# Attention by pairs of heads, with turned tiles by key block and the reciprocal applied at the gate

## The reference

```python
s_loc = einsum(qb, kb) * scale          # 8 heads of 64, blocks of 128 queries, 3 neighbouring blocks of 128 keys
s_loc = where(|qpos - kpos| <= 128 and key exists, s_loc, -1e30)
s_ctx = einsum(qb, kc) * scale          # 256 context keys
p = softmax(concatenate([s_loc, s_ctx, sink_l]))     # one sink value per head
o = einsum(p[..., :nloc], vb) + einsum(p[..., nloc:nloc + nctx], vc)
total = total + gates * ((ys[i] * silu(zs[i])) @ w_os[i])   # o is ys[0], silu(zs[0]) the attention gate
```

## Time and profile before

| | us |
|---|---|
| median of 3 runs | 2764.37 |
| lowest and highest | 2763.32, 2779.56 |
| the profiled execution | 2763.59 |
| its span, first to last instruction | 2761.8 |
| TensorE busy in it | 2550.7 (92%) |
| VectorE, ScalarE, GpSimd busy | 1139.5, 1114.2, 1355.2 |
| context attention, about 99 to 125 us | 26 |
| first latent attention, about 549 to 697 us | 148 |
| second latent attention, about 1752 to 1900 us | 148 |

### The profile page before, as it was taken

The page is one execution under the profiler, slowest core; times in us unless marked ns, Lnnn a source line. Parts: engine busy times, 40 slices in busy tenths (PEclk is TensorE's granted clock), DMA queues, the critical chain, the costliest instruction groups (busy, mean ns, idle before and its releaser), DMA issues.

```text
span 2761.8 us, 39510 instructions
## 1 busy us (share of the span) xinstructions
PE 2550.7 (92%) x13009; PEld 2117.8 (77%) x13009; DVE 1139.5 (41%) x1692; ACT 1114.2 (40%) x2229; POOL 1355.2 (49%) x1052
## 2 busy tenths in 40 slices
PE   7888968988999989999999979888999899999997
PEld 2777967787888767777888867777888688888886
DVE  2453346377153432333344366483344323233332
ACT  2644553277221454434433343574213433343332
POOL 1657962266221258864655442464222455555553
PEclk9899989999999999999999999999999999999999
DMA  5345661100121145543433431000210343344333
GB/s 229 96 117 175 190 191 50 42 1 1 47 65 33 32 126 160 158 139 126 148 108 107 144 114 43 16 1 28 61 40 24 89 120 109 109 133 146 113 107 121
DMA packets 392336, 266.44 MB, mean 96 GB/s; under 512 B 16263, under 2 KB 361495, under 8 KB 390683
## 3 DMA queue, kind: packets, MB, share of 16 engines
q1 hardware_dynamic: 379552, 231.26, 28.3%
q10 hardware_dynamic: 12668, 33.67, 3.4%
HBM read 255.42 MB, written 9.45 MB: 96 GB/s over the span
## 4 chain that ended last, share of the span: by engine, by line
PE 73%; issue 10%; POOL 7%; DVE 6%; ACT 3%; DMA 0%; ACTq 0%; POOLq 0%; DVEq 0%; SPq 0%
PE ps L639 71%; POOL w_lo L549 6%; DVE a_probT_lo L1532 2%; PE ps L786 1%; ACT a_probT_hi L1254 1%; DVE a_out_sum L1532 1%; DVE norm_tmp L1677 0%; DVE x_post L2074 0%; DVE hT_lo L1532 0%; PE ps L671 0%; DMA w_ada<-in_w_ada 0%; DVE r_prev L1873 0%; PE ps L738 0%; ACT a_prob L1243 0%; DVE x_post L1636 0%
## 5 line engine op out<-in xcount | busy, mean ns | idle before, releaser
L549 POOL TENSOR_TENSOR w_lo<-w_raw,w_hi 128x512 fp32r<-128x512 f32 x834 | 1126.3, 1361 | 1104.7 <-ACT w_hi L1081 1096.2
L639 PE MATMUL ps<-hT_hi,w_hi 128*128 128x512 f32 (+1 forms) x2528 | 948.0, 375 | 56.9 <-POOL w_lo L549 33.5
L1081 ACT ACTIVATE w_hi<-w_raw 128x512 fp32r<-128x512 f32 x834 | 519.0, 629 | 1029.2 <-PE ps L639 863.9
L639 PE MATMUL ps<-hT_hi,w_lo 128*128 128x512 f32 (+1 forms) x2528 | 934.2, 370 | 0.0
L639 PE MATMUL ps<-hT_lo,w_hi 128*128 128x512 f32 (+1 forms) x2528 | 934.2, 370 | 0.0
L639 PEld LDWEIGHTS ps<-hT_hi,w_hi 128*128 128x128 f32 x2528 | 483.3, 191 | 154.3 <-POOL w_lo L549 35.4
L639 PEld LDWEIGHTS ps<-hT_hi,w_lo 128*128 128x128 f32 x2528 | 483.4, 191 | 79.2
L639 PEld LDWEIGHTS ps<-hT_lo,w_hi 128*128 128x128 f32 x2528 | 484.0, 191 | 75.6
L1532 DVE TENSOR_TENSOR merge_tmp<-merge_tmp,ps 128x512 f32<-128x512 f32 (+1 forms) x160 | 101.5, 634 | 694.8 <-PE ps L639 437.7
L587 POOL TENSOR_TENSOR a_prob<-a_prob,softmax_stats 128x640 f32<-128x640 f32 (+2 forms) x144 | 163.5, 1135 | 142.8 <-DVE softmax_stats L1788 142.4
L1532 DVE TENSOR_TENSOR merge_tmp<-merge_tmp 128x512 f32<-128x512 f32 (+1 forms) x120 | 165.2, 1377 | 4.1
(11 more groups left out here) (243 smaller groups left out, 2804.0 us busy)
## 6 DMA issues: line engine op xcount, KB each, us to landing
w_raw<-in_w_in SPq DMA_DIRECT2D x512, 256.0 KB, 2.9
w_raw<-in_w_o_rest SPq DMA_DIRECT2D x120, 256.0 KB, 2.9
w_raw<-in_w_out SPq DMA_DIRECT2D x80, 256.0 KB, 2.8
w_ada<-in_w_ada SPq DMA_DIRECT2D x8, 1536.0 KB, 9.5
w_raw<-in_w_ada SPq DMA_DIRECT2D x48, 256.0 KB, 2.8
w_raw<-in_w_o_attn SPq DMA_DIRECT2D x40, 256.0 KB, 2.9
w_raw<-in_dft_x SPq DMA_DIRECT2D x32, 256.0 KB, 2.7
gate_row<-gate_rows ACTq DMA_DIRECT2D x5, 512.0 KB, 3.6
```

The lines of the kernel that those rows point to most:

```text
L549: eng.tensor_tensor(w_lo[:, r, :], raw[:, r, :], w_hi[:, r, :].bitcast(F32), ALU.subtract).then_inc(sem["w_split"], tally.up("w_split"))
L639: return eng.matmul(dst, lhsT, rhs, start=start, stop=stop)
L1081: return eng.activation(dst, src, func, **kw)
```

## The change

Pairs of heads take the place of single steps for everything behind the exponential. The probabilities are no longer scaled. The turned tiles of a pair go by key blocks into three banks: bank 4 holds blocks 0 and 1 of both heads, bank 5 blocks 2 and 3, and bank 6 block 4, where there is one. Each bank is called a chunk c, with its own semaphores (pT_turned, pT_high, pT_low) from TensorE to ScalarE to VectorE and back. VectorE writes the reciprocal of each row sum 64 times side by side (`one_over`, 128 columns for a pair), TensorE turns that tile into the other half of bank 6 (`turn_over`), ScalarE copies it out (`save_over`), and GpSimd multiplies it into the gate tile (weighed), and then the attention result (gated), two instructions of 128x256 for every two pairs. The values are multiplied one pair later than before. The low part of chunk 2 waits for `save_over` of its own pair too.

```diff
@@ -244,6 +244,8 @@
         o_sum = at("a_out_sum", [P, 2, 2, P], W + 17928)
+        over = [at("a_one_over_rows", [P, 4, P], C + 512), at("a_one_over_rows_ctx", [P, 4, P], W + 4096)]
+        over_cols = [at("a_one_over", [P, 2, P], C + 1024), at("a_one_over_ctx", [P, 2, P], W + 4608)]
         kc = at("a_kT_ctx", [P, 2, 2, CTX], Z + 2048, F32R)
@@ -389,17 +392,21 @@
             return [c for k in range(p.NT // 2) for c in (k, p.NT - 1 - k)]
-        def turned_at(n, count):
...
+        def key_blocks(p, qb):
+            return 2 if p.ctx else 5 - (qb == 0) - (qb == p.NT - 1)
+        def chunk(p, qb, c):
+            return max(min(key_blocks(p, qb) - 2 * c, 2), 0)
+        def heads_of(g):
+            return slice(2 * (g % 2), 2 * (g % 2) + 2)
+        def turned_chunk(c, blocks):
+            return ps[:, 4 + c, 0:blocks * 2 * P].rearrange("p (j h n) -> p j h n", h=2, n=P)
         def results(p, b):
@@ -570,25 +577,15 @@
             def attention(p):
-                groups = p.NT * 2
...
+                for g in range(p.NT * 2):
                     pair, qb = g // (p.NT // 2), 2 * (g % (p.NT // 2))
-                    eng.wait_ge(sem["out_sum"], tally.take("out_sum"))
                     zz = z_pass[p.s][:, qb // p.TB, Z_A + pair, (qb % p.TB) * P:(qb % p.TB + 2) * P].rearrange(
                         "p (a n) -> p a n", n=P)
+                    eng.wait_ge(sem["over_saved"], tally.take("over_saved", 2))
+                    eng.tensor_tensor(zz, over[p.s][:, heads_of(g), :], zz, ALU.mult).then_inc(sem["weighed"], tally.up("weighed"))
+                    eng.wait_ge(sem["weighed"], tally.now("weighed"))
+                    eng.wait_ge(sem["out_sum"], tally.take("out_sum"))
                     eng.tensor_tensor(zz, o_sum[:, g % 2, :, :], zz, ALU.mult).then_inc(sem["gated"], tally.up("gated"))
-
...
             def retention(p):
@@ -772,51 +769,67 @@
                     mm(ps[:, c + 1, 0:CTX], q, kc[:, kv, 1, :], False, True).then_inc(sem["score"], tally.up("score"))
-                def turn(n):
...
+                pairs, probs = len(steps) // 2, tally.now("prob")
+                def turn_over(g):
+                    eng.wait_ge(sem["one_over"], tally.take("one_over"))
+                    if tally.now("over_turned"):
+                        eng.wait_ge(sem["over_saved"], tally.now("over_turned"))
+                    if tally.now("pT_turned2"):
+                        eng.wait_ge(sem["pT_low2"], tally.now("pT_turned2"))
+                    eng.transpose(ps[:, 6, 2 * P:3 * P], over_cols[p.s][:, g % 2, :], ident[:, :]).then_inc(
+                        sem["over_turned"], tally.up("over_turned"))
+                def turn(g, c):
+                    blocks = chunk(p, steps[2 * g][0], c)
+                    if not blocks:
+                        return
+                    eng.wait_ge(sem["prob"], probs + 2 * g + 2)
+                    if tally.now(f"pT_turned{c}"):
+                        eng.wait_ge(sem[f"pT_low{c}"], tally.now(f"pT_turned{c}"))
+                    dst = turned_chunk(c, blocks)
+                    for j in range(blocks):
+                        for hh in range(2):
+                            w = slice((2 * c + j) * P, (2 * c + j + 1) * P)
+                            last = eng.transpose(dst[:, j, hh, :], prob[:, 2 * (g % 2) + hh, w], ident[:, :])
+                    last.then_inc(sem[f"pT_turned{c}"], tally.up(f"pT_turned{c}"))
+                def values(g, c):
+                    qb, h = steps[2 * g]
                     lo, hi = window(qb)
-                    places = turned_at(n, hi - lo + 2)
...
+                    kv, count = h // 4, hi - lo + 2
+                    if not chunk(p, qb, c):
+                        return
+                    if c == 0 and g % 2 == 0:
                         if tally.now("out_sum"):
                             eng.wait_ge(sem["out_sum"], tally.now("out_sum"))
                         tally.skip("out_sum", 1)
-                    dst, heads = ps[:, 7, pair * 2 * P:(pair + 1) * 2 * P], slice(2 * pair, 2 * pair + 2)
...
+                    eng.wait_ge(sem[f"pT_low{c}"], tally.take(f"pT_low{c}"))
+                    dst = ps[:, 7, g % 2 * 2 * P:(g % 2 + 1) * 2 * P]
+                    for j in range(2 * c, 2 * c + chunk(p, qb, c)):
                         v = vx[:, lo + j, kv, :, :] if j < hi - lo else vc[:, j - (hi - lo), kv, :, :]
-                        mm(dst, v, pT_hi[:, j, heads, :], j == 0, False)
...
+                        mm(dst, v, pT_hi[:, j, heads_of(g), :], j == 0, False)
+                        last = mm(dst, v, pT_lo[:, j, heads_of(g), :], False, j == count - 1)
+                    if g % 2 and 2 * c + chunk(p, qb, c) == count:
                         last.then_inc(sem["pv"], tally.up("pv"))
                 eng.wait_ge(sem["a_split"], tally.take("a_split"))
-                scores(0)
...
+                for g in range(pairs + 3):
+                    if g < pairs:
+                        scores(2 * g)
+                    if g > 2:
+                        values(g - 3, 0)
+                        values(g - 3, 1)
+                    if g < pairs:
+                        scores(2 * g + 1)
+                    if g > 2:
+                        values(g - 3, 2)
+                    if 0 < g <= pairs:
+                        turn_over(g - 1)
+                        turn(g - 1, 2)
+                        turn(g - 1, 0)
+                        turn(g - 1, 1)
             def late_keys(p):
@@ -1246,13 +1259,21 @@
                         sink_column(n + 2)
-                def save(n):
...
+                weighed = tally.now("weighed")
+                def save(g, c):
+                    blocks = chunk(p, steps[2 * g][0], c)
+                    if blocks:
+                        eng.wait_ge(sem[f"pT_turned{c}"], tally.take(f"pT_turned{c}"))
+                        eng.activation(pT_hi[:, 2 * c:2 * c + blocks, heads_of(g), :], turned_chunk(c, blocks), ACT.Copy).then_inc(
+                            sem[f"pT_high{c}"], tally.up(f"pT_high{c}"))
+                def save_over(g):
+                    eng.wait_ge(sem["over_turned"], tally.take("over_turned"))
+                    if g > 3:
+                        eng.wait_ge(sem["weighed"], weighed + g // 2 - 1)
+                    act(over[p.s][:, g % 4, :], ps[:, 6, 2 * P:3 * P]).then_inc(sem["over_saved"], tally.up("over_saved"))
                 def low_half():
@@ -1269,16 +1290,21 @@
                 sink_column(1)
-                exps(0)
...
+                pairs = len(steps) // 2
+                for g in range(pairs + 3):
+                    if g < pairs:
+                        exps(2 * g)
+                    if g > 2 and g % 2 == 0:
                         low_half()
-                save(len(steps) - 1)
...
+                    if 0 < g <= pairs:
+                        save(g - 1, 2)
+                    if g < pairs:
+                        exps(2 * g + 1)
+                    if 0 < g <= pairs:
+                        save(g - 1, 0)
+                        save_over(g - 1)
+                        save(g - 1, 1)
+                tally.skip("weighed", pairs // 2)
             def decay_tables():
@@ -1782,19 +1807,25 @@
                         sem["max"], tally.up("max"))
-                def one_over(n):
...
+                turned, saved = tally.now("over_turned"), tally.now("over_saved")
+                def one_over(g):
+                    eng.wait_ge(sem["prob"], tally.take("prob", 2))
+                    if g > 1:
+                        eng.wait_ge(sem["over_turned"], turned + g - 1)
+                    eng.reciprocal(over_cols[p.s][:, g % 2, :].rearrange("p (h d) -> p h d", d=HD),
+                                   soft[:, heads_of(g), 1:2].to_broadcast([P, 2, HD])).then_inc(sem["one_over"], tally.up("one_over"))
+                def low(g, c):
+                    blocks = chunk(p, steps[2 * g][0], c)
+                    if blocks:
+                        eng.wait_ge(sem[f"pT_high{c}"], tally.take(f"pT_high{c}"))
+                        if c == 2:
+                            eng.wait_ge(sem["over_saved"], saved + g + 1)
+                        high = pT_hi[:, 2 * c:2 * c + blocks, heads_of(g), :].bitcast(F32)
+                        tt(pT_lo[:, 2 * c:2 * c + blocks, heads_of(g), :], turned_chunk(c, blocks), high, ALU.subtract).then_inc(
+                            sem[f"pT_low{c}"], tally.up(f"pT_low{c}"))
                 def add_halves(g):
@@ -1813,20 +1844,24 @@
                    vc[:, :, :, 0, :].bitcast(F32), ALU.subtract).then_inc(sem["a_split"], tally.up("a_split"))
-                groups = len(steps) // 4
...
+                pairs, groups = len(steps) // 2, len(steps) // 4
+                for g in range(pairs + 3):
+                    if 1 < g <= pairs + 1:
+                        low(g - 2, 2)
+                    if g < pairs:
+                        maximum(2 * g)
```

(67 more changed lines are left out.)

45 lines of the change are left out of this document (2 added, 43 removed).

## The result

The changed kernel takes 2832.47 us (median of 4 runs, 2822.72 to 2836.01), the kernel before 2763.85 us (4 runs, 2762.47 to 2779.56). The ratio is 1.0229, with a 95% interval of 1.0185 to 1.0274: slower, and the forecast of 2831 us is met within 2 us. The profiled execution is the fastest of the four, 2822.7 us; the other three, at 2831 to 2836 us, have a mean granted clock of 0.966 to 0.967 in place of 0.973. So the profile shows 59 of the 69 us.

What follows compares the result with a forecast made beforehand. No engine was full; a closed ring through VectorE and ScalarE, 5.69 us a pair, was to bound the changed kernel. 54 + 6 + 4 + 3 = +67 on 2763.6 us gave 2831 us, own range 2808 to 2850, 8-in-10 range 2788 to 2862.

Steps and rivals of the forecast that it cites:

- The stall before and what could be won: Latent passes before the change: 0.7 us of stall a pair, 45 us over 64 pairs, all that better overlap can win.
- The reciprocal's price: VectorE's reciprocal, widened from 1 to 128 columns, takes 0.95 us.
- The ring: VectorE's low parts, maxima and reciprocal, then ScalarE's exponential and copies, back to chunk 2's low part: 5.69 us a pair.
- The columns: Each column of 8 pairs in the latent passes takes 42.5 us against 35.7: +54 us in all.
- The context pass: Context attention, no chunk 2: reciprocal, turning, scores, maximum and low part take 3.1 to 3.3 us a pair, +6 us.
- The +3 for the clock: TensorE drops to 1.2 GHz after the new waits, mostly absorbed by 1.8 us of idle time a pair: +3 us.
- the first rival: TensorE's clock stays low for a third or more of the pairs: +35 us, 2866 us, chance 0.14.
- The +4 for hand-overs left out: Hand-overs missing from the column sums, 0.5 us for each of 8 latent columns: +4 us.
- A reciprocal as cheap as other operations: Rival 2: VectorE's wide reciprocal costs 0.42 us, ring 5.16 us, total 2790 us, chance 0.10.
- The third rival: VectorE's wait before chunk 2's low part never closes the ring, reciprocal cheap, TensorE the bound: about 2735 us, chance 0.05.
- The fourth: All rings slack, VectorE's own work of 4.30 us a pair is the bound: no change, 2765 us, chance 0.05.

Runs made afterwards that it cites:

- narrow reciprocal: The changed kernel with a reciprocal of 2 columns and a VectorE copy spreading them to 128, order kept: 2787.0 us, 1.0086 of the kernel before.
- double reciprocal: The changed kernel with the 128-column reciprocal made twice, one behind the other: 2900.8 us, 1.0502 of the kernel before.
- low part behind the maximum: The changed kernel with VectorE's low part of chunk 2 moved behind the pair's first maximum: 2789.2 us, 1.0077 of the kernel before.
- early copy-out: The changed kernel with ScalarE copying out the turned reciprocal right behind chunk 2, ahead of the second exponential: 2773.8 us, 1.0048 of the kernel before.
- both: The changed kernel with the early copy-out and the narrow reciprocal together: 2733.0 us, 0.9901 of the kernel before.
- with GpSimd: The changed kernel with early copy-out and 2-column reciprocal, the copy that spreads it moved from VectorE to GpSimd: 2737.0 us, 0.9887 of the kernel before.

## Why the prediction was right

**The stall before and what could be won: right in kind, put too high.** The prediction put TensorE's own work at 3.72 us for an inner pair (3.83 with the turned reciprocal) and 3.1 for an outer one, 29.2 us a column, and the stall at 45 us in all. With ring and wide reciprocal out of the way a column takes 32.0 us, 4.0 a pair, and TensorE is full. So its work was sized some 7 to 10% too low, and what was won is 29 us. The windows spoke for that already: 126 us busy in the four columns of the first latent attention are 31.6 us a column.

**The reciprocal's price: right.** 0.942 us against 0.95, worked out by the slope between 8 and 32 columns. The slope holds to 128 columns: (0.942 - 0.352) / 96 = 6.1 ns a column.
**The ring: right, 2% too long.** 5.56 us against 5.69. Three pieces differ by the starts in the timeline: the low part behind the reciprocal takes 0.54 (taken 0.60); the exponential lets the copy behind it start after 0.78 us (taken 0.88, which counted the read-out of the sum); the copy of the reciprocal with its hand-over takes 0.38 (taken 0.32). Three experiments show the ring itself: opening it took 57 us away without removing work, shortening it with the narrow reciprocal left it closed at 5.10 us (5.05 by the sum), and the double reciprocal made it 6.55. The run with the low part behind the maximum fits it, but fits the second ring as well. That second ring, through TensorE's transposes and scores, is in no part of the prediction. In the change it is slack, so the forecast did not need it; it takes over, with VectorE's own work, as soon as the first is open.

**The columns: right, 10% too much.** 41.8 us against 42.5, +49 us for eight of them against +54; outer pairs turn in 4.34 us, given as 4.4. The context pass: +5 in the profiled execution against +6. Some of the signs were set a little too high: the column was to take 42 to 44 us, the latent attention 174 to 182 (it took about 169 and 174), TensorE's wait 1.5 to 1.9 us a pair (1.3 on average).

**The two small terms: not as argued.** The +3 for the clock rested on TensorE falling to 1.2 GHz at its new waits of 1.3 us. It did not: the mean granted clock of the first latent stretch is 0.98 against 0.97 before, and 1.00 in its middle, so the first rival, and the Trainium skill's warning about short idling in "TensorE: Matmul & The Clock Gate", section "A second HAM failure mode: psum-queue depth-cycling", did not come true in the changed kernel. It did in part in the double reciprocal, where the waits are 2.1 us a pair: the granted clock there is 0.90 and 0.94, so the rival was nearer than the changed kernel alone shows. The +4 for hand-overs left out is not there either; the columns came out shorter than the sum. Against that, 7 us outside the attention stretches in the profile, and about 10 more in the other three executions at a lower clock, were in no term. Errors of opposite sign made the total agree better than its parts: the profiled execution is +59 against the sum's +67, which was made for it. That the median came within 2 us of 2831 is luck; the mechanism is not.

**The rivals.** A reciprocal as cheap as other operations is out at 0.94 us. The third rival named the right place and the right condition: with the wait ahead of the low part no longer late and the reciprocal cheap, the two together, TensorE becomes the bound and the kernel is faster. Its time (2733 measured, 2735 given) agrees by luck: a column too short (29.2 us against 32.0), with half of its gain struck off for hand-overs. Its point of decision was right too, that neither alone wins. The fourth, VectorE's own work as the bound with about 2765 us, is about what the early copy-out alone reaches, at 2774, with the second ring holding part of the pairs.

What stays open is the part that lies outside the eight columns. Between profiled executions (the last column of the table less eight times that of the column) it is 10 us for the change, 7 for the early copy-out and for the narrow reciprocal, -5 for both, 16 for the double reciprocal, 12 for the low part behind the maximum and 9 with GpSimd. So it does not follow the length of the ring. Much of it arises early. In the change the first product of projections behind the context attention starts 5 us later than before, and the 93 us of projections behind that add nothing. In the early copy-out it starts 6 us later, and the same projections, which no edit touches, take 4 us more; their mean granted clock is 0.84, against 0.90 in the kernel before and 0.91 in the change. No run shows why the clock is lower there, nor why three of four executions of the change have a mean clock 0.006 to 0.007 below the profiled one.

## What to carry to other kernels

When work is rearranged between engines, follow each semaphore once round, from an instruction through everything queued ahead of it on each engine and back to itself: no iteration can be shorter than the longest such ring, however free the engines look. A wait at the head of an engine's iteration on something that another engine does at the end of its own closes such a ring, and moving one short instruction forward opens it. Then look for the next ring: here one of 4.49 us stood behind the one of 5.56. A period that agrees with the sum of one ring does not show that this ring holds; see which wait is left. And before a per-row value is widened so that it can be turned, price the operation that widens it: compute it narrow and spread it with a copy.

## What the runs showed of the hardware

VectorE's reciprocal costs 6.1 ns a column up to 128 columns (0.942 us), where the same engine copies 128 columns with broadcast in 0.227 us and GpSimd in 0.292 us. TensorE, waiting 1.3 to 1.6 us once in most pairs of about 5.5 us, kept a granted clock of 1.00, 2.4 GHz, through the middle of the pass. With the reciprocal doubled it waited up to 2.6 us in pairs of 6.6 us, and the mean granted clock of the first latent attention fell to 0.90. In the kernel before, a wait of 1.70 us near the end of the first latent attention was followed by 1.2 GHz, while one of 1.71 us at the same place of the second was followed by a granted clock of 1.00 (window 1895.5 to 1898.5).
